# Storing the expert rows of a one-core mixer and MoE layer: from two engines' copies and a 32-partition store to one copy and a 128-partition store

## The reference

```python
hg = jnp.einsum('td,edf->tef', xt, p['w_gate'])
hu = jnp.einsum('td,edf->tef', xt, p['w_up'])
act = jax.nn.silu(hg) * hu * gates[:, :, None].astype(x.dtype)
return jnp.einsum('tef,efd->td', act, p['w_down']).reshape(bsz, seq_len, d)
```

## Time and profile before

| What | us |
|---|---|
| median of 3 runs | 931.18 |
| profiled execution, device time | 929.58 |
| its span | 927.8 |
| expert stage, first `gate_and_up` to the last store landed | 612 to 887 |
| after it, gather and combine | 887 to 927.8 |

### The profile page before, as it was taken

The page is one execution under the profiler, slowest core; times in us unless marked ns, Lnnn a source line. Parts: engine busy times, 40 slices in busy tenths (PEclk is TensorE's granted clock), DMA queues, the critical chain, the costliest instruction groups (busy, mean ns, idle before and its releaser), DMA issues.

```text
span 927.8 us, 17180 instructions
## 1 busy us (share of the span) xinstructions
PE 819.1 (88%) x6827; PEld 445.4 (48%) x6827; DVE 409.9 (44%) x799; ACT 269.5 (29%) x539; POOL 108.3 (12%) x210
## 2 busy tenths in 40 slices
PE   3789989999999999999998999369999999999900
PEld 1223355555455456655664455335555555555500
DVE  5345541221384293375453774733333333333335
ACT  1367331211111110327222233113333333333332
POOL 3000000000001000000001000022222222222140
PEclk9899899999999999999999999579999999999965
DMA  8996010421602602023107203899999999996162
GB/s 255 413 386 242 0 35 1 182 103 78 242 31 77 197 3 91 23 72 133 24 1 267 96 24 113 330 415 423 416 416 421 416 421 421 415 419 258 40 237 113
DMA packets 40202, 191.40 MB, mean 206 GB/s; under 512 B 4417, under 2 KB 4713, under 8 KB 32530
## 3 DMA queue, kind: packets, MB, share of 16 engines
q1 hardware_dynamic: 28426, 152.50, 40.9%
q0 software_dynamic: 9168, 31.61, 10.0%
q10 hardware_dynamic: 2552, 6.50, 1.9%
HBM read 174.14 MB, written 16.44 MB: 205 GB/s over the span
## 4 chain that ended last, share of the span: by engine, by line
PE 81%; DVE 6%; DMA 5%; ACT 4%; issue 2%; SPq 1%; POOL 0%; DVEq 0%; ACTq 0%; POOLq 0%
PE banks L1905 19%; PE banks L1579 15%; PE banks L1916 9%; PE banks L1809 4%; PE banks L1580 4%; PE banks L1819 4%; PE banks L1540 3%; PE banks L1620 3%; PE banks L1715 3%; DMA arena<-in_w_ada 3%; PE banks L1724 2%; PE banks L1472 2%; ACT arena L752 2%; PE banks L1518 2%; PE banks L1672 1%
## 5 line engine op out<-in xcount | busy, mean ns | idle before, releaser
L1905 PE MATMUL banks<-arena 128*32 128x256 f32 x3072 | 177.1, 383 | 5.0 <-DVE arena L1394 5.0
L1579 PE MATMUL banks<-arena 128*128 128x512 f32 x320 | 164.2, 595 | 2.6 <-ACT arena L705 1.6
L1905 PEld LDWEIGHTS banks<-arena 128*32 128x32 f32 x3072 | 96.1, 110 | 68.9 <-issue 6.6
L1580 PEld LDWEIGHTS banks<-arena 128*128 128x128 f32 x320 | 60.8, 190 | 76.5 <-issue 76.5
L1394 DVE STREAM_TRANSPOSE arena<-arena 128x256 f32<-128x256 f32 x49 | 32.3, 660 | 139.2 <-PE banks L1905 135.7
L1916 PE MATMUL banks<-arena 128*32 128x256 f32 x1536 | 91.7, 379 | 1.0 <-DVE arena L1418 1.0
L1916 PEld LDWEIGHTS banks<-arena 128*32 128x32 f32 x1536 | 50.0, 110 | 33.8 <-DVE arena L1418 1.2
L1580 PE MATMUL banks<-arena 128*128 128x128 f32 x320 | 61.5, 274 | 0.0
L1401 DVE COPY arena<-banks 32x256 f32<-32x256 f32 x98 | 41.4, 422 | 40.4 <-PE banks L1916 39.7
L845 ACT ACTIVATE arena<-banks 32x256 f32<-32x256 f32 x98 | 36.8, 375 | 71.4 <-PE banks L1916 70.9
L1579 PEld LDWEIGHTS banks<-arena 128*128 128x128 f32 x320 | 48.5, 192 | 6.1 <-issue 4.9
(11 more groups left out here) (375 smaller groups left out, 992.1 us busy)
## 6 DMA issues: line engine op xcount, KB each, us to landing
arena<-in_w_gate SPq DMA_DIRECT2D x16, 2048.0 KB, 22.4
arena<-in_w_up SPq DMA_DIRECT2D x16, 2048.0 KB
arena<-in_w_down SPq DMA_DIRECT2D x16, 2048.0 KB
arena<-in_w_ada SPq DMA_DIRECT2D x12, 2048.0 KB, 15.0
arena<-in_w_in SPq DMA_DIRECT2D x7, 2048.0 KB, 7.8
expert_output<-arena ACTq DMA_DIRECT2D x49, 128.0 KB
expert_output<-arena POOLq DMA_DIRECT2D x1, 4096.0 KB, 20.4
arena<-in_w_out SPq DMA_DIRECT2D x2, 2048.0 KB, 8.0
```

The lines of the kernel that those rows point to most:

```text
L1579: M(ps[:, b, :], lhs, hT[:, k, CTX:TOK], start=k == 0, stop=k == KD - 1)
L1580: mm = M(ps[:, b + 1, 0:CTX], lhs, hT[:, k, 0:CTX], start=k == 0, stop=k == KD - 1)
L1905: mm = M(ps[q * LANE:(q + 1) * LANE, 2, 0:2 * P].rearrange("p (g f) -> p g f", g=2), xg[:, k, :], gate_up[e % 3][:, :, k, q * P:(q + 1) * ...
```

## The change

The copy out of bank 5 becomes one DVE instruction over all 128 partitions and 256 columns. `ysb` has the bank's shape now: partition 32 q + r holds quarter q of row r. ACT copies nothing; it waits for the DVE copy and issues the store, whose DRAM side is walked as 4 quarters, 32 rows, 256 columns (1 KB runs), and whose SBUF side as 128 partitions. The semaphore `y_a` is gone, and with it one wait of `down` on PE. The wait for `y_stored` is on DVE alone.

```diff
--- before.py
+++ after.py
@@ -276,7 +276,7 @@
     fold, used, t_coef = area(W6 + 512, P), area(W6 + 640, NE, NT + 1), area(W6 + 736, NE, NT + 1)
     e_coef, g_coef, cum = area(W6 + 832, NT, NE), area(W6 + 912, NT, NG), area(W6 + 932, NE + 1)
     w12 = rt(2, NT)
-    ysb = [area(bufr[0] + i * D, D, rows=LANE) for i in range(2)]
+    ysb = [area(bufr[0] + i * D, D // LANES) for i in range(2)]
     phot, early, later = rt(2 * NT, LANE), rt(2 * NT, EARLY), rt(2 * NT, GROUPS + 2 - EARLY)
     parts = rt(GROUPS + 2)
     rt(2 * D - 2 * NT * (LANE + GROUPS + 2) - GROUPS - 2)
@@ -301,7 +301,7 @@
         e_ready w_ready s_done p_ready kw_ready inter_done inter_read intra_done num_ready upd_done st_ready
         h_ready hsq hss hrs yml_ready yt_done yt_read wo_done wo_sq wo_ss wo_rs x2_sq x2_rs h2_ready h2t_done h2t_read
         lg_done rt_v rt_exp pos_done idx_done tiles_ready route_ready
-        idx_taken xg_ready gu_done silu_ready act_ready at_t aT_d down_done y_a y_d
+        idx_taken xg_ready gu_done silu_ready act_ready at_t aT_d down_done y_d
         comb_s comb_v comb_rs fin_ready act_chain dve_chain pool_chain""".split()
     S = {n: sem(n) for n in names}
     ld_max = [sem(f"ld_max{i}") for i in range(2)]
@@ -837,20 +837,15 @@
 
         act.wait_ge(S["tiles_ready"], 2)
 
-        def y_out(i, n, stores):
-
-            act.wait_ge(S["down_done"], i + 1)
-            act.wait_ge(y_stored[n], stores)
-            for l in range(2):
-                ins = act.activation(ysb[n][:, l * 256:(l + 1) * 256], ps[l * LANE:(l + 1) * LANE, 5, 0:256], ACT.Copy)
-            ins.then_inc(S["y_a"], 1)
-            act.wait_ge(S["y_a"], i + 2)
+        def y_out(i, n):
+
             act.wait_ge(S["y_d"], i + 2)
             row = nc.s_assert_within(i, 0, GROUPS,
                                      skip_runtime_bounds_check_because="at most GROUPS groups in all") * LANE
-            act.dma_start(y_dram[bass.ds(row, LANE), :], ysb[n]).then_inc(y_stored[n], 16)
-
-        start_at_one(act, "silu_ready", "y_a")
+            act.dma_start(y_dram[bass.ds(row, LANE), :].rearrange("r (q c) -> q r c", q=LANES), ysb[n])\
+                .then_inc(y_stored[n], 16)
+
+        start_at_one(act, "silu_ready")
         for n in range(2):
             act.sem_inc(y_stored[n], 16)
         pairs = act.value_load(tiles_i[0:1, 16:17], min_val=MINGROUPS // 2, max_val=GROUPS // 2)
@@ -862,10 +857,10 @@
                 act.wait_ge(S["gu_done"], i + 1)
                 act.wait_ge(S["act_ready"], i)
                 act.activation(gact, ps[:, 2, 0:P], ACT.Silu).then_inc(S["silu_ready"], 1)
-                y_out(i - 1, n, 16 * pair + 16)
+                y_out(i - 1, n)
 
         pairs = act.value_load(tiles_i[0:1, 16:17], min_val=MINGROUPS // 2, max_val=GROUPS // 2)
-        y_out(2 * pairs, 0, 16 * pairs + 16)
+        y_out(2 * pairs, 0)
         act.wait_ge(y_stored[0], 16 * pairs + 32)
         act.wait_ge(y_stored[1], 16 * pairs + 16)
         link(A(st1[:, 70:71], epsc, ACT.Copy), "all_stored")
@@ -1397,9 +1392,7 @@
 
             dve.wait_ge(S["down_done"], i + 1)
             dve.wait_ge(y_stored[n], stores)
-            for l in range(2, LANES):
-                ins = dve.tensor_copy(ysb[n][:, l * 256:(l + 1) * 256], ps[l * LANE:(l + 1) * LANE, 5, 0:256])
-            ins.then_inc(S["y_d"], 1)
+            dve.tensor_copy(ysb[n], ps[:, 5, 0:256]).then_inc(S["y_d"], 1)
 
         start_at_one(dve, "act_ready", "xg_ready", "xg_ready", "aT_d", "y_d")
         turn_rows(0, 16)
@@ -1909,7 +1902,6 @@
         def down(i, e):
 
             pe.wait_ge(S["aT_d"], i + 1)
-            pe.wait_ge(S["y_a"], i + 1)
             pe.wait_ge(S["y_d"], i + 1)
             for q in range(FF // P):
                 for l in range(LANES):
```

## The result

The changed kernel takes 1007.78 us (median of 4 runs, 998.42 to 1013.37) against 931.13 for the kernel before in the same comparison: ratio 1.0811, interval 1.0766 to 1.0856, slower by some 76 us. 1017 was predicted, with the likeliest case's own range from 970 to 1080. The profiled execution is the quickest of the four, 998.42 us, span 996.6; before it was 927.8, so the profile has 68.8 us to account for.

A forecast was written before the change was run, and what follows sets the result against it. PE was taken to set the end, with the DMA engines right behind it. Copies -0.9, stores +81, clock +5 and last store +1.2 gave +86 on the profiled 929.58, 1016, and 1017 as median; range 960 to 1075 at 0.77.

The forecast's parts named there:

- the likeliest case: Four engines carry each store, piece by piece: 1017 us, own range 970 to 1080, chance 0.74.
- The four engines: New store, 128 outermost in SBUF and 4 in DRAM: only 4 engines, 32 pieces each, 132 packets a store.
- The turns: Store packets alternating with weight packets: 33 turns of 0.66 us, 22 us beside gate and up, where 12.5 are allowed.
- Capacity: Four engines' time: 1.58 us a store each in place of 0.34, 20.9 us an expert against PE's 16.7.
- The lower bound of +43: Expert stage, stores filling every gap: 4.2 us for each of 13 experts, 54 us, less 11: +43 us.
- The term of +81: Expert stage slowed by stores on four engines: 22.9 us an expert, 13 x 6.2 = +81 us.
- the clock's: PE's granted clock falling after stops, three or four such restarts: +5 us (0 to 15).
- The copies' -0.9: One DVE copy in place of two, counting twice at the end, at the last down and last store: -0.9 us.
- Sixteen engines: Rival: all 16 engines carry the store, nine turns, only the copies' saving stays: 930.3 us, chance 0.10.
- Bundling by four: Rival: four engines, pieces bundled by four, nine turns, only engine time counts: +43, 974 us, chance 0.10.
- Half-rate writes: Rival: 16 engines, but small writes at half rate, 0.79 us a store: about +11, 942 us, chance 0.03.
- Faster: Rival: store on 16 engines, and PE's dropped wait had cost 0.1 us a group: -4.8 - 0.9, 925.5 us, chance 0.03.

The follow-up runs named there:

- Experiment 2: Changed kernel with the store's DRAM side walked as 128 contiguous pieces, so 128 outermost on both sides and 16 engines; 928.71 us, ratio 0.9992.
- experiment 5: Changed kernel with its store cut into four quarter stores on 16 engines each, and four half-size buffers in place of two; 929.71 us, ratio 0.9973.
- experiment 3: Kernel before, its copies and 4 KB pieces kept, with the store's DRAM side walked as 4 x 8 rows, so four engines; 958.14 us, ratio 1.0307.
- experiment 7: Changed kernel with its store cut into two stores of two quarters each, 2 outermost on the DRAM side; 1053.04 us, ratio 1.1274.
- experiment 1: Changed kernel with its store cut into four quarter stores, 32 outermost on both sides, 16 engines each, two buffers kept; 946.83 us, ratio 1.0156.
- experiment 4: Changed kernel with gate and up weights read in 4 KB runs in place of 16 KB; 980.73 us, ratio 1.0532.
- experiment 6: Changed kernel, its one store on 4 engines kept, with four half-size buffers in place of two; 982.88 us, ratio 1.0544.

## Why the prediction was right, and where its sizes were off

**The four engines: right.** 132 packets a store were named and came. Experiment 2 undoes this (and the order of the addresses, which experiment 5 clears) and the loss goes; experiment 3 does this one thing to the kernel before and a loss comes. The rule of the Trainium skill (DMA: Bandwidth & Descriptors, section "Why a DMA increments its semaphore by 16 and not by 1"), the largest count up to 16 that divides the outermost sizes of both sides, now has unequal sizes to stand on: 128 and 4 gave 4 completions (132 packets), 32 and 4 gave 4 (36), 128 and 128 gave 16 (144), 64 and 2 gave 2 each. That the engines are the same ones from store to store, experiment 7 shows by its time.

**The turns: right in kind, the price too high.** 33 turns were put at 22 us for a store by itself. On the chain a store takes 13.9 to 25.2 us, but that holds the wait for the store ahead: the 25.2 are nearly two stores' packets. By itself the first store took 18.3, and one that had another ahead of it landed up to 14.0 us behind that one (638.96, 645.71, 659.66, 671.59, the copies that the landings released). The error stands in the prediction: 33 x 0.66 wants 33 long packets beside the store, and its own upper bound counts 16 long and 32 short ones an expert. By that count a store is at most 16 x 0.66 + 17 x 0.21 = 14.1 us, an estimate that the first store still exceeds. That 14.1 is also over the 12.5 allowed, so the stop was forecast rightly, with less to spare. Nine and twelve turns fell on the two sides of the edge that the prediction's price gives (experiments 1 and 2). That DVE would stop in `y_out`, with `aT`, `down` and the next group behind it, is the chain of the timeline.

**Capacity: right in size, wrong in how it shows.** 1.58 us a store and engine were predicted, 1.52 measured, and the estimate of 100% for the four engines fits it. The lower bound of +43, where only capacity counts, lies near what the change costs with 4 KB weight runs, 47 with some 6 either way. But I had PE wait for weights too; in the changed kernel it never did. The loads came early (median landing of the gate weights 9.6 us from 620 to 900 us, in place of 26.0 before, from 620 to 850). That fits a PE that is held up by the stores and frees the slots late, when the queue is short; no run shows it by itself. The weights became late where the stores were on time or nearly so (experiments 3 and 4).

**The term of +81 was mis-sized,** and the clock's too, in opposite directions. In the profiled execution the waits added 52 us, 4.0 for each of 13 experts where I had 6.2. The clock added 16.5, over its range of 0 to 15: I had counted three or four restarts and there were 15 waits in front of `down`, some at half clock like the 3.64 us above. Together 69 against 86. The price of a turn is one reason to have sized the waits too high; 22.9 us an expert was a choice between two bounds, and the lower one was nearer. The median lies 9 us higher than that execution, and no profile shows which of the two terms those are; the mean granted clock of the four runs falls as their time grows, from 0.935 at 998.42 us to 0.921 at 1013.37.

**Small terms.** The new copy 0.425 us (0.43 predicted), the last store +1.3 (+1.2), its issue 0.55 us in place of 0.33 (+0.3 at most was allowed for). The copies' -0.9: in experiment 2 it is the 0.5 us at the last `down`, and from there to all stored 2.6 us in place of 3.5.

**The rivals.** Sixteen engines: excluded by 132, and its price of 930.3 was borne out by experiment 2, at 928.71. Bundling by four: excluded, since 32 data packets would show and 128 do. Half-rate writes: excluded by 6.1 us for 132 packets, 46 ns each. *Faster* had 0.1 us a group hidden in PE's wait for `y_a`: experiment 5, which has the new copy and no loss, is 2.0 us under the kernel before, not 5.7. By its interval it gains 0.4 to 4.6 us, 0.9 of which are the copies, so at most 3.7 of the 4.8 us can have been hidden there.

## What to carry to other kernels

Before changing the shape of a DMA, write down the outermost count of both its sides: the greatest count up to 16 that divides both is the number of engines, and packets less data packets in the profile confirm it. In a stage whose DMA engines are full, price a store per engine, not over all, and its landing packet by packet: its packets on one engine, each with one of the other queue beside it, and no more long ones than that queue has in a row. Add the stores that are still ahead of it in its own queue, and compare this with the time until its buffer is wanted. Several issues with a good count on both sides beat one with a bad one, but they take turns too, and may want more buffers. More buffers alone don't cure a full engine: the wait can come back at the issue.

## What the runs showed of the hardware

- The same 128 pieces of 1 KB landed in 9.4 us (median of experiment 2) or took 13.9 to 25.2 us (the stores on the changed kernel's chain beside weight loads), by 128 or 4 outermost on the DRAM side.
- Issuing it took ACT 0.55 us (4 x 32 x 256 against 128 partitions) in place of 0.32, 0.34 with 128 outermost (experiment 2), and four issues of a quarter each took 1.75. With more stores under way on few engines single issues took up to 10.36 us (experiment 6) and 7.88 us (experiment 7).
- The changed kernel spread over 15 us in four runs; experiments 4, 6 and 7, with the same kind of store, over 3 to 5 us each. Why is open.
- Gate and up weights in 4 KB runs in place of 16 KB cost 0.2%, and its interval, 0.9997 to 1.0052, includes no cost at all.
